# Layer 0's attention in a two-block transformer kernel: where four gate tiles and two modulation units stand among its steps

## The reference

```python
mod = silu_c @ w_mod[l] + b_mod[l]          # 6 vectors of 1024; mod_c likewise from c_ctx
sh1, sc1, g1, sh2, sc2, g2 = jnp.split(mod[:, None, :], 6, axis=-1)
h = modulate(rms_norm(x, norm1[l]), sh1, sc1)
na_q, na_k, na_v, gq, gk, gv, ga, gb = jnp.split(h @ w_in[l], IN_SPLITS, axis=-1)
ya = merge_heads(na_latent(qa, ka, va, ka_c, va_c, bias, row_idx))        # 8 heads, a window plus the context
ob = gqa_latent(qb, k_all, v_all)                                         # 8 heads, 2 key heads, rms_norm and rope on q, k
x = x + g1 * branch_merge(ya, yb, ga, gb, w_pa[l], w_pb[l], w_o[l])       # sigmoid(ga) * (ya @ w_pa) + sigmoid(gb) * (yb @ w_pb)
```

## Time and profile before

| | us |
|---|---|
| median of 3 runs | 2548.78 (2548.51 to 2551.3) |
| the profiled execution's own time | 2548.03 |
| its span | 2546.2 |
| PE busy in it | 2460.0 |
| part of the span in which layer 0's attention steps run (start of S(0) to end of the last V) | 130.9 to 364.4 |

### The profile page before, as it was taken

One profiled execution on the slowest core, in us unless ns is written; L12 is line 12 of the kernel. 1 busy time (PEld: TensorE's weight loads), 2 busy tenths in 40 slices (PEclk: granted clock), 3 DMA queues, 4 the chain that ended last, 5 costly groups with the idle time before them and its releaser, 6 DMA issues.

```text
span 2546.2 us, 41010 instructions
## 1 busy us (share of the span) xinstructions
PE 2460.0 (97%) x17036; PEld 2202.9 (87%) x17036; DVE 1426.9 (56%) x2394; ACT 1133.0 (44%) x1960; POOL 360.8 (14%) x354
## 2 busy tenths in 40 slices
PE   7988999999999999999999998999999999999998
PEld 4754778888888877899999998999999998899998
DVE  4135335574456445555566567576556556657654
ACT  3244443422222535554454444465445444447443
POOL 0233313100001315200100000240000000024000
PEclk9998999999999999999999999999999999999999
DMA  7632123354444322345565453355455454335544
GB/s 283 217 98 97 55 81 132 116 173 135 156 166 165 137 96 84 133 166 177 171 210 185 164 167 119 128 179 182 167 190 190 167 190 138 115 125 196 182 163 136
DMA packets 82697, 390.32 MB, mean 153 GB/s; under 512 B 14992, under 2 KB 23472, under 8 KB 52176
## 3 DMA queue, kind: packets, MB, share of 16 engines
q1 hardware_dynamic: 73136, 347.78, 40.0%
q0 software_dynamic: 9376, 39.91, 4.5%
HBM read 386.62 MB, written 1.05 MB: 152 GB/s over the span
## 4 chain that ended last, share of the span: by engine, by line
PE 86%; DVE 6%; ACT 5%; issue 2%; DMA 1%; POOL 0%; SPq 0%; DVEq 0%; POOLq 0%; ACTq 0%
PE ps L1111 74%; PE ps L1292 2%; DVE ring_lo L1983 2%; PE ps L1370 2%; PE ps L1355 2%; PE ps L1344 1%; ACT logits L1718 1%; ACT w_hi L1513 1%; PE ps L1205 1%; ACT prob_t L1725 0%; DMA arena<-w_mod 0%; PE ps L1144 0%; PE ps L1305 0%; DVE arena L2465 0%; PE ps L1176 0%
## 5 line engine op out<-in xcount | busy, mean ns | idle before, releaser
L1983 DVE TENSOR_TENSOR ring_lo<-ring,w_hi 128x1024 fp32r<-128x1024 f32 (+3 forms) x704 | 763.5, 1125 | 328.7 <-ACT w_hi L1513 328.6
L1111 PE MATMUL ps<-h_hi,w_hi 128*128 128x256 f32 (+1 forms) x3392 | 937.0, 308 | 3.9 <-issue 1.6
L1111 PE MATMUL ps<-h_lo,w_hi 128*128 128x256 f32 (+1 forms) x3392 | 924.1, 304 | 1.5 <-DVE h_lo L2158 1.5
L1513 ACT ACTIVATE w_hi<-ring 128x1024 fp32r<-128x1024 f32 (+3 forms) x704 | 633.3, 947 | 410.9 <-PE ps L1111 374.0
L1111 PEld LDWEIGHTS ps<-h_hi,w_hi 128*128 128x128 f32 x3392 | 648.6, 192 | 45.4 <-issue 18.4
L1111 PEld LDWEIGHTS ps<-h_lo,w_hi 128*128 128x128 f32 x3392 | 648.9, 192 | 26.2 <-DVE h_lo L2158 1.7
L1111 PE MATMUL ps<-h_hi,ring_lo 128*128 128x256 f32 (+1 forms) x3392 | 558.1, 303 | 2.5 <-DVE ring_lo L1983 2.5
L1111 PEld LDWEIGHTS ps<-h_hi,ring_lo 128*128 128x128 f32 x3392 | 480.8, 192 | 27.4 <-DVE ring_lo L1983 3.0
L1111 PE MATMUL ps<-hid_hi,w_hi 128*128 128x256 f32 (+1 forms) x1078 | 290.1, 299 | 0.0
L1111 PE MATMUL ps<-hid_lo,w_hi 128*128 128x256 f32 (+1 forms) x1078 | 289.5, 298 | 0.0
L1910 POOL TENSOR_SCALAR logits<-logits,stat 128x512 f32<-128x512 f32 (+2 forms) x140 | 161.3, 1165 | 590.2 <-DVE stat L2349 590.2
(11 more groups left out here) (285 smaller groups left out, 2403.1 us busy)
## 6 DMA issues: line engine op xcount, KB each, us to landing
ring<-w_ffn_in SPq DMA_DIRECT2D x132, 1024.0 KB, 4.9
ring<-w_ffn_out SPq DMA_DIRECT2D x96, 704.0 KB, 4.0
ring<-w_in SPq DMA_DIRECT2D x36, 1024.0 KB, 4.9
ring<-w_w_in SPq DMA_DIRECT2D x28, 1024.0 KB, 5.0
bias_t<-w_mod POOLq DMA_DIRECT2D x24, 1024.0 KB, 5.4
ring<-w_up SPq DMA_DIRECT2D x16, 576.0 KB, 3.7
ring<-w_mod SPq DMA_DIRECT2D x8, 1024.0 KB, 5.6
ring<-w_pab SPq DMA_DIRECT2D x8, 1024.0 KB, 4.9
```

Source lines behind the costliest of these rows:

```text
L1111: mm = pe.matmul(ps[fs[k].bank][:, at_col:at_col + n], (hi_w if wpart == "hi" else lo_w)[0:rows, at[k]:at[k] + P], hi if part == "hi" else ...
L1513: act.activation(w_hi[q.s % 2][:, h * n:(h + 1) * n], ring[q.slot][:, h * n:(h + 1) * n], ACT.Copy)\
L1983: dve.tensor_tensor(ring_lo[q.slot][:, c], ring[q.slot][:, c], plain(w_hi[q.s % 2][:, c]), ALU.subtract)\
```

## The change

Unit 1 leaves the `nak` and `gvf` tiles and POOL's queue. Its pieces come through the ring, two after each of steps 5, 6, 7 and 8, with the turn right behind the last two. Then a gate tile follows steps 9, 11, 13 and 15 (gates 12 to 15, each from a piece of its own with half the columns, 512 KB), and two pieces of unit 2 follow steps 10, 12, 14 and 16, with the turn behind the last. `run_all(*nk)` puts the `nak` tiles back to back. The 12 other gates are spread over the 19 calls of steps 17 to 35: none after 17, 19, 22, 25, 27, 30 and 33, one after each of the others, in the order 0 to 3, 8 to 11, 4 to 7. `held` keeps the PSUM bank in which a unit is being summed from being handed out by `linear()`. The item `ahead` that stood before the first gate is gone.

```diff
--- before.py
+++ after.py
@@ -144,7 +144,7 @@
     def __init__(self):
         self.items, self.pieces, self.splits = [], [], []
         self.full, self.taken, self.lin, self.counts = [0] * 8, [0] * 8, 0, {}
-        self.in_slot = [0] * RING
+        self.in_slot, self.held = [0] * RING, None
 
     def add(self, kind, **kw):
         self.items.append(dict(kind=kind, **kw))
@@ -157,6 +157,8 @@
 
     def linear(self):
         self.lin += 1
+        if (self.lin - 1) % LIN == self.held:
+            self.lin += 1
         return self.fill((self.lin - 1) % LIN)
 
     def piece(self, src, length, split=True):
@@ -351,7 +353,7 @@
                 else:
                     m.update(p=piece(mod_src(l, j, c), SLOT, False))
                 yield m
-            add("mod_turn", l=l, j=j, of=f, f=f2 or fill(TURN_BANK))
+            add("mod_turn", l=l, j=j, of=f, f=f2 or linear())
 
         def mod_half(l, j, c):
             n, h, k = 4 * j + c // 4 * 2, c % 4 // 2, c % 2 * 2 * 512
@@ -697,7 +699,11 @@
                 yield add("gv", f=feats["gv", 0], after=feats["gvf", 0])
 
             gate_tiles = []
-            for u in range(8):
+            if l == 0:
+                for c in range(12, 16):
+                    half = f[7 + c // 2].rearrange("p (k n) -> p k n", k=KC)[:, :, c % 2 * P:c % 2 * P + P]
+                    gate_tiles.append(feat("gate", half, [c], T, length=KC * P, l=l))
+            for u in range(8) if last else (0, 1, 4, 5, 2, 3):
                 gate_tiles.append(feat("gate", f[7 + u], [2 * u, 2 * u + 1], T, l=l))
 
             def gate():
@@ -707,18 +713,12 @@
 
             gates = gate()
             if l == 0:
-                unit, loads = mod_unit(0, 1, True), mod_loads(0, (1,), (logits, prob_t), turned)
-                some(loads, 2)
                 first_tiles_out(first)
-                in_turn(unit, loads, 2)
-                for t in nk:
-                    for i, _ in enumerate(t):
-                        in_turn(unit, loads, 1 + i)
+                run_all(*nk)
                 add("tables", n=1, after=feats["nak", 0])
                 add("na_bias", l=0, n=0, after=feats["nak", 0])
                 vals = values()
                 next(vals)
-                some(unit, 1)
                 tok("nav", w["w_nav"][l], 2, SLOT, 512, SQ, nav)
                 next(vals)
                 g = attention([na_pair(i, 0, 0, SQ) for i in range(4)] + [na_pair(i, S, S, S) for i in range(4)])
@@ -726,39 +726,58 @@
                     for _ in t:
                         att(g)
                 hn = head_norm(norm_chunks(), "sum_heads", hroot)
-                unit = mod_unit(0, 2, f=linear(), f2=linear())
+
+                def mods(unit, last=False):
+                    some(unit, 2)
+                    if last:
+                        plan.held = None
+                        some(unit, 1)
+
+                def held_unit(j):
+                    f = linear()
+                    plan.held = f.bank
+                    return mod_unit(0, j, f=f)
+
+                unit = held_unit(1)
                 head_squares(hn, 0, 1, 2, 3)
                 att(g)
-                some(unit, 1)
+                mods(unit)
                 head_squares(hn, 4)
                 att(g)
-                some(unit, 1)
+                mods(unit)
                 head_sums(hn)
                 att(g)
-                some(unit, 1)
+                mods(unit)
                 att(g)
-                some(unit, 1)
+                mods(unit, True)
                 head_spread(hn, 0, 1, 2)
                 att(g)
-                some(unit, 1)
+                unit = held_unit(2)
+                next(gates)
                 head_spread(hn, 3, 4)
                 att(g)
-                some(unit, 1)
+                mods(unit)
+                att(g)
+                next(gates)
                 rope(ropes[:3], 1, need=(hn["last"],))
                 add("keys_swap", n=plan.counts["rope"] - 2)
                 att(g)
-                some(unit, 1)
+                mods(unit)
                 rope(ropes[3:], 1, need=(hn["last"],))
                 att(g)
-                some(unit, 1)
-                add("ahead", p=plan.pieces[-1])
-                last_mod = unit
+                next(gates)
+                att(g)
+                mods(unit)
+                att(g)
+                next(gates)
                 g2 = attention([gq_pair(i, 0, 0, SQ) for i in range(4)] + [gq_pair(i, S, S, S) for i in range(4)])
                 g["steps"] += g2["steps"]
                 att(g)
-                some(last_mod, 1)
-                while g["i"] < 19:
+                mods(unit, True)
+                left, tiles = len(g["steps"]) + 4 - g["i"], 12
+                for i in range(left):
                     att(g)
+                    some(gates, (i + 1) * tiles // left - i * tiles // left)
             else:
                 next(q[0])
                 for a in nxt:
```

## The result

| | before | after |
|---|---|---|
| median of 20 runs, us | 2548.65 (2545.34 to 2551.68) | 2553.30 (2549.75 to 2556.11) |
| ratio after / before | | 1.0019, 95% interval 1.0014 to 1.0025 |
| span of the profiled execution | 2546.2 | 2551.3 |

The change made the kernel 4.7 us slower. The forecast was 11.0 faster, 2537.8, with a range of 2530 to 2546, and the time lies 15.5 above it. The prediction called 5.1 either way no change and gave that band 0.17; slower than that had 0.04, and any time outside the range 0.18.

What follows compares the result with a forecast made beforehand. PE, busy for 97% of the span, bounds the kernel, so only waits and lower-clock time can be won. Losses of 27.8 for 35.4 before, plus part 1's 3.4, gave 11.0 faster: 2537.8 us, range 2530 to 2546.

Steps and rivals of the forecast that it cites:

- part 3: Gates after steps 9, 11, 13, 15: PE waits 3.3 at gate 12, 1.2 elsewhere, 1.3 at the second turn; splits inside gates free.
- Rival C: Steps 6 to 9: the ring doesn't keep up with two modulation pieces a step; 18 us, giving 2555.8; chance 0.05.
- A: Rival: the clock falls again and again, after steps 5 to 8 and gateless steps; 11.5 more, 2549.3; chance 0.09.
- B: Rival: gateless steps cost little, 3 in place of 12.4, and one clock fall; gain 22, 2526.8; chance 0.08.
- D: Rival: order doesn't matter as PE's busy time is the same; only part 1's 3.4 gained, 2545.4; chance 0.10.
- Part 1: Unit 1 out of the `nak` tiles: what follows starts 12.2 earlier, 8.8 of it work that returns, 3.4 won.
- Part 2: Two pieces after steps 5 to 8: second hides in waits, leaving 0, 0.8 and 0.8; the turn waits 0.9.
- Gate 12: The gate after step 9, not split ahead: PE waits 3.3 for `w_hi`.
- Part 4: Gates spread over steps 17 to 35: seven gateless steps lose 12.4 in all; bounds 3 and 18.
- The clock: Two falls, around the first turn and at gate 12, 3.0 in all; 1.00 from gate 12 on.

Runs made afterwards that it cites:

- e1: Changed kernel with the splits of gates 13 to 15 and of the first 1 MB gate piece moved behind the modulation pieces of steps 10, 12, 14, 16: 2542.85 us.
- e7: Changed kernel with each of unit 2's eight pieces loading only its first quarter, 256 KB for 1 MB, order and splits kept: 2541.63 us.
- e4: Kernel before with unit 1 moved alone, unit 2's pieces after steps 9 to 12, no gate tile before step 19: 2544.73 us.
- e9: e2 with its twelve late gates in one run after steps 17 to 28 and none after 29 to 35: 2533.04 us.
- e2: e1 with gate 12 split ahead as well, behind the last pair of unit 1's pieces: 2539.12 us.
- e5: e2 with the twelve late gates in one run from step 24 on, steps 17 to 23 bare: 2540.79 us.
- e10: e2 unchanged, timed again in the same group as e9: 2539.36 us.

## Why the prediction was wrong

**The step that failed** is in part 3: "Gates 13 to 15 and the first of the others are split inside the gate before them", costed at nothing, and "What waits behind ACT's wait for gate 13's landing is gate 12's copy out and the exponentials of step 10; both have 5.67." It named the wait for the landing and the queue behind it, at nothing for gate 13 and at 0.4 for gate 15, and the only landing that it had was the 5.6 of the earlier trace rows. Four things were missed. A gate's piece starts only when the gate before it begins, the one with the split in it. Its landing with two others ahead is 7.1 to 8.7. A tile gives only 5.67 of cover, and ACT reached the split 7.25 and 5.22 too early in gates 13 and 15. And behind ACT's half comes DVE's half, and behind that on DVE's queue stand the rope work and the copy to `row`, for which PE waits. In gates 12 and 14 ACT waited nearly as long, 5.09 and 4.77. Behind the first PE lost nothing. Behind the second it lost 0.26 ahead of S(15) and 0.71 ahead of T(13), to which the chain of waits leads from that split, and e1 has neither. So the wait's length alone doesn't tell its price. The prediction gave the second turn 0.9 and 0.4 for this; it cost 3.30, and the rope product, with 1.2 for all such waits, 4.99.

**What it was worth.** e1 takes it away by order and wins 10.5 by medians, e7 by shorter transfers ahead and wins 11.7. The traces put 8.6 and 9.1 between the start of gate 12 and that of gate 0: the two waits shrink by 4.99 - 0.18 and 3.30 - 0.93 in e1, small waits elsewhere take 1.6 of that back, and 3.0 is instructions that ran slow. So 9 to 12 of the 15.5 is this cause, shown twice. With it gone e1 stands at 2542.85, 5.0 above the forecast. In that rest are step 17, where e1 waits 1.99 and S(18) takes 2.59 for 1.13 (3.5, forecast 1.5), and the clock at gate 12 and ahead of it (below). How the rest divides was not tried apart.

**Rival C** had the right cause, the landing, with 0.05 and the wrong engine: it asked whether PE's own pieces come late. They hardly do, at 7.0 for a piece: 1.70 in e4, and not at all in the changed kernel. What comes late is the piece behind them that ACT and DVE must split. Its price of 18 was near the 15.5 by accident.

**The other rivals.** A's sign was a low clock behind the gateless steps; from 264.05 to 363.94, where six of the seven stand, it is 0.99. B's sign was no waits there; there are 7.6. D, that the order doesn't matter, falls with e9. The chances that the prediction adds up for "faster" make 0.77, not 0.79.

**Part 1** was right and small by 2. `nav` starts at 88.74 (forecast 90.8), 14.2 earlier than the end of that stretch in the earlier trace rows; the 8.8 of moved work taken off, 5.4 is won where 3.4 was forecast (0.8 of it ahead of the first `nak` tile, which starts at 61.54). The five tiles took 27.20, 5.44 each rather than 5.67. e4 confirms the sign: 4.2 faster as a whole.

**Part 2** was right on every wait: 0.62 ahead of the head sums and 0.92 ahead of S(8) for 0.8 each, 0.84 ahead of the turn for 0.9. The clock was not foreseen: it was low at V(5) and T(6) (0.62 from 173.52 to 178.05), back at 1.00 for the two pieces and the turn, and low again from S(9) at 185.37 into the first part of gate 12; 145.20 to 191.35 has 0.89.

**Gate 12**: its wait was forecast 3.3 and is 2.86, for the reason given. The tile then took 7.25 for 5.67, as its first matmuls take 0.63 where 0.40 is the full clock's. That clock was not the wait's doing: it was at 0.50 from S(9) on, before the wait, and e2, without the wait, has slow matmuls there too. e2 takes the wait away and wins 3.7.

**Part 4, the steps without a gate**: 19, 22, 25, 27, 30 and 33 were forecast at 10.9 and lost 10.5: 7.6 of waits and 2.9 in groups of instructions right behind them that took longer than in a filled step. The sum is right, its parts less so: the waits ahead of S are 0.3 to 0.8 as forecast, those for ACT's copy 0.45 to 0.71 where 1.3 was forecast, and the one behind step 33 is 2.03 for 0.9. Two of them, changed kernel, PE in time order:

```profile
295.37 1.73 PE L1363 MATMUL ps<-arena 64*128 64x512 f32 x4 [0.82 <-DVE logits L2356]
297.77 1.07 PE L1374 MATMUL ps<-con,logits 128*128 128x128 f32 x8 [0.66 <-ACT prob_t L1744]
...
362.03 1.98 PE L1389 MATMUL ps<-prob_t,arena 128*64 128x256 f32 x8 [2.03 <-DVE prob_t L2381]
```

The bound of 2.7 each from the bare stretch of before was not reached: e5 has seven in a row, at 1.9 for a long one (S(20) at 253.15 to S(22) at 262.66 less 5.65 of work, halved 1.9).

**The clock** was the other term that was mis-sized. The forecast was two falls, 3.0 in all, and 1.00 from gate 12 on. Measured is a mean of 0.93 over 218.74 us, about 31 us at 1.2 GHz. The rule weighed there, from the Trainium skill ("TensorE: Matmul & The Clock Gate", "PE-mode transpose"), that transposes don't count as activity, would have brought a fall in the steps without a gate. It didn't come: e5's seven steps, each with a T, keep 0.96. In the changed kernel the two falls that cost most follow the long waits of PE, the 4.99 and the 3.30. The one at S(9) doesn't: the waits just ahead of it are 0.84 before the turn and 0.16 before a spread, and S(9) takes 1.23 for 0.70 in every trace here, that of the kernel before among them. The fall at V(5) is a third case. V(5) in e2 and in e10, the same kernel:

```profile
171.39 3.04 PE L1395 MATMUL ps<-prob_t,arena 128*64 128x256 f32 x16 [0.88 <-ACT prob_t L1750]
```

```profile
171.57 1.95 PE L1395 MATMUL ps<-prob_t,arena 128*64 128x256 f32 x16 [0.88 <-ACT prob_t L1750]
```

It took 3.00 to 3.61 in the changed kernel, e2, e4 and e7, and 1.95, the full clock's time, in the eight others. So the same waits take the clock down in one execution and not in another. Why, stays open, and why the bare steps had 0.65 in the kernel before and 0.59 in e4 where e5's have 0.96.

**A slip**: "The last V ends about 353.5" left out that one more gate tile stands behind the last V than before; with it the forecast was 347.8. It ended at 363.94, 16.1 later, about the miss of the whole.

## What to carry to other kernels

A wait on an in-order engine costs what stands behind it, not what it guards: when a load is placed early, ask for every engine that touches it what is queued behind that touch, and put the touch behind the last thing that others wait for. The Trainium skill says that ScalarE's and VectorE's queues are strictly first in, first out ("TensorE: Matmul & The Clock Gate", "Architectural detail: the array is 16× 32×32, not 1× 128×128"); here what stood behind two waits was worth some 10 us. Take a transfer's landing time with the bytes that will be started ahead of it, not from a row in which it runs alone, and ask what lets it start. And filler work went better into a run, with the last steps left bare, than evenly (2533.0 against 2539.4): the same matmuls in three orders took 2553.3, 2539.1 and 2533.0.

## What the runs showed of the hardware

- A 512 KB piece started 2.3 us after the first of two 1 MB pieces on SP's queue landed 8.7 us after its start; one with nothing started in the 11 us ahead of it 4.1. Behind 256 KB pieces in place of the 1 MB ones such pieces took 4.3 in the median (e7). The 26 pieces of 1 MB of `w_w_in` took 4.9 in the median.
- Rows of 512 bytes instead of 4096 changed ACT's total wait by 1.4 of 22.3 and the median landing from 5.8 to 6.8, and the time not at all (2552.7 and 2553.3).
- Seven attention steps in a row, with a first wait of 2.4 and then waits of 0.3 to 0.9 us, kept a mean clock of 0.96 (e5), while the stretches around one wait of 5.0 and one of 3.3 had 0.79 and 0.72 (changed kernel).
- In one and the same kernel, after the same waits, a group of 16 matmuls took 3.04 in one execution (e2) and 1.95 in another (e10).
